# Memory tokens and the first key weights loaded in halves of the summed dimension, in a two-layer encoder step

## The reference

```python
def mem_kv(mem, norm_g, wk, wv, k_norm_g):
    bsz, m, _ = mem.shape
    hm = rmsnorm(mem, norm_g)
    mk = rmsnorm((hm @ wk).reshape(bsz, m, MEM_HEADS, MEM_HEAD_DIM), k_norm_g)
    mv = (hm @ wv).reshape(bsz, m, MEM_HEADS, MEM_HEAD_DIM)
    return mk, mv
```

## Time and profile before

| | us |
|---|---|
| median of 3 runs | 1813.92 |
| lowest, highest | 1813.88, 1814.5 |
| span of the profiled execution | 1812.1 |
| TensorE busy in it | 1766.3 (97%) |
| VectorE busy | 888.0 (49%) |
| ScalarE busy | 510.9 (28%) |
| GpSimd busy | 159.2 (9%) |

### The profile page before, as it was taken

One profiled execution on the slowest core, in us unless ns is written; L12 is line 12 of the kernel. 1 busy time (PEld: TensorE's weight loads), 2 busy tenths in 40 slices (PEclk: granted clock), 3 DMA queues, 4 the chain that ended last, 5 costly groups with the idle time before them and its releaser, 6 DMA issues.

```text
span 1812.1 us, 27654 instructions
## 1 busy us (share of the span) xinstructions
PE 1766.3 (97%) x11792; PEld 1608.6 (89%) x11792; DVE 888.0 (49%) x1398; ACT 510.9 (28%) x791; POOL 159.2 (9%) x153
## 2 busy tenths in 40 slices
PE   7999998999999999999999999899999999999997
PEld 6566556988999999999999997699799999999997
DVE  3699857557544323444335135644764442244431
ACT  4111254354322111122232144533442111111211
POOL 3011101221000000000023132100110000000000
PEclk9999999999999999999999998999999999999999
DMA  7222420251311122221223224213232112222120
GB/s 252 99 78 92 112 100 7 105 205 64 116 69 55 64 101 71 76 72 48 94 94 49 93 70 177 99 48 140 94 124 85 62 48 87 93 70 82 51 91 31
DMA packets 32059, 161.61 MB, mean 89 GB/s; under 512 B 8600, under 2 KB 9240, under 8 KB 18032
## 3 DMA queue, kind: packets, MB, share of 16 engines
q1 hardware_dynamic: 24032, 121.97, 20.1%
q0 software_dynamic: 7952, 38.60, 6.0%
HBM read 149.87 MB, written 10.42 MB: 88 GB/s over the span
## 4 chain that ended last, share of the span: by engine, by line
PE 93%; DVE 3%; ACT 1%; issue 1%; DMA 0%; POOL 0%; SPq 0%; DVEq 0%; ACTq 0%
PE G L798 88%; PE S L798 2%; PE Q L798 2%; PE Q L1408 1%; ACT work L1494 1%; ACT rstd L1494 0%; DMA ring<-in_w_mk 0%; DVE ev_low L2267 0%; DVE stats L2297 0%; PE Q L1205 0%; DVE stats L2563 0%; DVE work L2310 0%; DVE rstd L2018 0%; ACT mkT L1494 0%; ACT front L1494 0%
## 5 line engine op out<-in xcount | busy, mean ns | idle before, releaser
L798 PE MATMUL G<-h_split,w_split 128*128 128x320 f32 x5184 | 763.6, 309 | 0.0
L798 PEld LDWEIGHTS G<-h_split,w_split 128*128 128x128 f32 x5184 | 760.6, 188 | 0.2 <-issue 0.2
L1494 ACT ACTIVATE w_split<-ring 128x1024 fp32r<-128x1024 f32 (+2 forms) x172 | 165.0, 961 | 750.0 <-PE G L798 750.0
L798 PE MATMUL G<-g_split,w_split 128*128 128x320 f32 x2112 | 310.4, 309 | 0.0
L798 PEld LDWEIGHTS G<-g_split,w_split 128*128 128x128 f32 x2112 | 309.9, 188 | 0.0
L798 PE MATMUL G<-front,ring 128*128 128x128 f32 (+2 forms) x832 | 222.2, 428 | 11.2 <-DMA ring<-in_w_mk 9.4
L2033 DVE TENSOR_TENSOR w_split<-ring,w_split 128x1024 fp32r<-128x1024 f32 (+2 forms) x154 | 166.8, 1084 | 132.4 <-ACT w_split L1494 132.1
L798 PEld LDWEIGHTS G<-front,ring 128*128 128x128 f32 x832 | 132.2, 192 | 99.8 <-issue 96.0
L2410 DVE TENSOR_TENSOR work<-work,G 128x640 f32<-128x640 f32 x44 | 36.1, 821 | 204.1 <-PE G L798 204.1
L2108 DVE SCALAR_TENSOR_TENSOR front<-front,par 128x512 f32<-128x512 f32 x240 | 113.6, 547 | 0.1
L2401 DVE TENSOR_TENSOR work<-G,rstd 128x640 f32<-128x640 f32 x44 | 36.3, 824 | 128.7 <-PE G L798 116.2
(11 more groups left out here) (310 smaller groups left out, 1765.2 us busy)
## 6 DMA issues: line engine op xcount, KB each, us to landing
ring<-in_w_up0a SPq DMA_DIRECT2D x11, 1024.0 KB, 4.9
ring<-in_w_up0b SPq DMA_DIRECT2D x11, 1024.0 KB, 4.9
ring<-in_w_up1a SPq DMA_DIRECT2D x11, 1024.0 KB, 4.9
ring<-in_w_up1b SPq DMA_DIRECT2D x11, 1024.0 KB, 4.8
front<-in_mem_k POOLq DMA_DIRECT2D x8, 1024.0 KB, 7.2
front<-in_mem_v POOLq DMA_DIRECT2D x8, 1024.0 KB, 11.4
ring<-in_w_down0a SPq DMA_DIRECT2D x8, 704.0 KB, 4.0
ring<-in_w_down0b SPq DMA_DIRECT2D x8, 704.0 KB, 4.1
```

The costliest lines, as they stand in the source:

```text
L798: return nc.tensor.matmul(out, lhsT, rhs, start=start, stop=stop, **kw)
L1494: return nc.scalar.activation(*a, **k)
```

## The change

SyncE issues `par` first, then the first half of the tokens (steps 0 to 3) and the first half of key chunk 0 (the columns of the same steps, 4 KB per partition), then both second halves, then the early constants; x and the rest follow as before. The two halves of the tokens have semaphores of their own (`mem_in[0]`, `mem_in[1]`), the first half of the chunk has `half_in`, the second raises the chunk's usual one. TensorE runs the first four steps of tile 0 and of tile 1 when the first halves are there, then the last four of each. PSUM holds both tiles meanwhile. The wait for `ones` moves to the statistics after tile 1. ScalarE and VectorE wait for each half of the tokens when they come to it.

```diff
@@ SyncE
-            sp.dma_start(memx, dram["mem"]).then_inc(mem_in, 16)
+            def first_half(i):
+
+                ks = slice(4 * i, 4 * i + 4)
+                sp.dma_start(memx[:, ks], dram["mem"][:, ks]).then_inc(mem_in[i], 16)
+                at = slice(i * WCH // 2, (i + 1) * WCH // 2)
+                sp.dma_start(ring[:, 0, at], dram[CHUNKS[0][0]][0][:, at]).then_inc(chunk_in[0] if i else half_in, 16)
+
+            sp.dma_start(par[:, :], dram["par"]).then_inc(par_in, 16)
+            first_half(0)
+            first_half(1)
             sp.dma_start(const[:, 0:EARLY], dram["const"][:, 0:EARLY]).then_inc(ones_in, 16)
-            sp.dma_start(par[:, :], dram["par"]).then_inc(par_in, 16)
...
-            load(0, slice(0, 1), None)
             for k in range(0, KD, 2):
                 sp.dma_start(x[:, k:k + 2, :], dram["x"][:, k:k + 2, :]).then_inc(x_in[k // 2], 16)
             load(1, slice(1, 2), None)
@@ TensorE
-            pe.wait_ge(ones_in, 16)
...
+            def first_keys():
+
+                for half in range(2):
+                    if half:
+                        chunk(0)
+                    else:
+                        pe.wait_ge(half_in, 16)
+                    for n in range(2):
+                        out = G[n] if half else begin(n)
+                        for k in range(4 * half, 4 * half + 4):
+                            if n == 0:
+                                pe.wait_ge(mem_scaled, k + 1)
+                            m = mm(out[:, 0:MT], ring[:, 0, k * 256 + n * P:k * 256 + n * P + P], memh[:, 0, k, :],
+                                   k == 0, k == KD - 1)
+                        if half:
+                            m.then_inc(tile_done, 1)
+
             def memory_keys(l):
+                if l == 0:
+                    first_keys()
                 for n in range(4):
-                    if n % 2 == 0:
+                    if n % 2 == 0 and (l or n):
                         s = chunk(CHUNK[f"mk{l}"] + n // 2)
-                    project(TILE0[f"mk{l}"] + n, s, n % 2 * P, KD, lambda k: memh[:, l, k, :], width=MT,
-                            normed=1 if l and n == 0 else None, scaled=mem_scaled if l == 0 and n == 0 else None)
+                    if l or n >= 2:
+                        project(TILE0[f"mk{l}"] + n, s, n % 2 * P, KD, lambda k: memh[:, l, k, :], width=MT,
+                                normed=1 if l and n == 0 else None)
                     if l == 0 and n == 1:
+                        pe.wait_ge(ones_in, 16)
                         total = rstd[:, nstat[0] % 2, :]
@@ ScalarE
-            act.wait_ge(mem_in, 16)
             for k in range(KD):
+                act.wait_ge(mem_in[k // 4], 16)
                 square(memx[:, k, :], MT)
@@ VectorE
-            dve.wait_ge(mem_in, 16)
             for k in range(KD):
+                dve.wait_ge(mem_in[k // 4], 16)
                 v.tensor_scalar(memh[:, 0, k, :], memx[:, k, :], pr("mem0", k), None, ALU.mult).then_inc(mem_scaled, 1)
```

More of the change, by code:

```diff
@@ L484, in build @@
         h_hi, q_eps, silu = map(sem, ("h_hi", "q_eps", "silu"))
-        ones_in, const_in, par_in, mem_in, pads_in = map(
-            sem, ("ones_in", "const_in", "par_in", "mem_in", "pads_in"))
+        ones_in, const_in, par_in, half_in, pads_in = map(
+            sem, ("ones_in", "const_in", "par_in", "half_in", "pads_in"))
+        mem_in = [sem(f"mem_in{i}") for i in range(2)]
         x_in = [sem(f"x_in{i}") for i in range(KD // 2)]
@@ L808, in begin, with project @@
                 return G[n % 2]
-            def project(n, wslot, col, KT, rhs, cols=256, width=T, normed=None, halfway=None, scaled=None):
+            def project(n, wslot, col, KT, rhs, cols=256, width=T, normed=None, halfway=None):
                 out = begin(n)
@@ L817, in project @@
                         pe.wait_ge(applied, normed + k)
-                    if scaled is not None:
-                        pe.wait_ge(scaled, k + 1)
                     w = ring[:, wslot, k * cols + col:k * cols + col + P]
```

## The result

| | median us | lowest to highest | runs |
|---|---|---|---|
| before | 1814.01 | 1813.1 to 1817.44 | 18 |
| with the change | 1818.04 | 1815.64 to 1821.65 | 18 |

The ratio is 1.002, with an interval of 1.0013 to 1.0027: about 4 us slower, against a forecast of 1814.0 and a range up to 1816.0. The spread has grown too: 17 of the 18 runs of before lie within 1.7 us, those of the change over 6 us. The profiled execution has a span of 1816.2 us, 4.1 above that of before.

A forecast was written before the change was run, and what follows sets the result against it. The wait for value chunk 1, last late before 28.74 us in a backed-up load queue, was taken to absorb the earlier start. Span 1812.1 + 0.1 for halves = 1812.2, plus 1.8 from span to median: 1814.0 us, range 1812.2 to 1816.0.

The forecast's parts named there:

- The main step: At the first value product: TensorE waits for value chunk 1, landing at 28.6 us, so an earlier start gains nothing.
- the cost of halves in the queue: Loads at the start: halves cost -0.6 to +0.4 us, taken as +0.1, going straight into value chunk 1's landing.
- The sentence on the skill's rule: Load queue: the skill's about 2 us per transfer has no room as a serial cost; x's four parts took 6.37 us.
- The start: First product of key tile 0: at 6.5 us (6.2 to 7.5) instead of 9.42, with 1152 KB less ahead of it.
- I keep 8.83 us: First two key tiles: the same 16 steps keep their slow start-up and take 8.83 us, 6.5 to 15.3.
- the lead: TensorE's gain on the kernel before: 2.9 us at tile 1, 1.6 at key tile 2, zero at the value products.
- The gap: TensorE's idle time ahead of the first value product, waiting for value chunk 1: 2.4 us in place of 0.97.
- The clock: Rival: longer idle before 28.7 us may halve TensorE's granted clock, costing 1.65 us, to 1815.7; chance 0.10.
- the row at 42.8 us: Profile of the kernel before: after a single 1.8 us idle ahead of 42.88 us the granted clock stayed at 1.00.
- The rival on each transfer's cost: Rival: two more transfers in the queue put the end up to 3.2 us later, 1817.1, or 1817.5; chance 0.03.
- SyncE's two more issues: Ahead of x and later loads: 0.44 us each, so these are issued 0.9 us later, costing nothing.
- the earlier issue of `glu`: Next weight chunk after tile 1: issued at 15.3 us in place of 18.28, still behind the value chunks, costing nothing.

The follow-up runs named there:

- filler: Changed kernel with four extra products, results unused, in TensorE's idle time ahead of the value products: 1816.17 us.
- after_repeat: The changed kernel run once more, nothing altered: 1818.72 us, ratio 1.0018 to the kernel before.
- whole_4k_rows: order_only with tokens and key chunk 0 in one transfer each, cut into 256 rows of 4 KB by the DRAM layout: 1814.10 us.
- order_only: Kernel before with the change's order of loads alone, tokens and key chunk 0 whole, no halves: 1813.91 us, ratio 0.9998.
- late_halves: order_only with key chunk 1, not chunk 0, in two half transfers at every other 4 KB of DRAM: 1814.95 us.
- halves_contiguous: Changed kernel with tokens and key chunk 0 laid out in DRAM so each half is one unbroken 512 KB piece: 1815.25 us.

## Why the prediction was wrong

**The main step held.** "Whatever it does earlier ends in this same wait": with value chunk 1 ahead of x the gap vanished in all four runs with that move, and only then did an earlier first product bring the statistic of x forward with it.

**The step that failed is the cost of halves in the queue**, -0.6 to +0.4 us. It measured +1.57 at the value products in the profiled execution and more in the others (filler 2.0, after_repeat 2.9), and +2.3 in the median of the runs with a mean granted clock of 0.995 or more. I priced the halves by the length of a row alone, from whole loads with rows of 5 and 3.6 KB; whole_4k_rows shows that this comparison was right and beside the point. Transfers were counted at nothing, from x in four parts at full rate, but those were parts of a load that was in four parts anyway, each with its own rows side by side. That a half reads every other 4 KB of the array was in the diff, and no row of before has such a load; it should have kept a bound of its own. The sentence on the skill's rule went too far as well: a serial 2 us for each transfer is not seen, but splitting did cost with unbroken halves too, 0.23 and 0.47 MB in two executions. And a loss in bytes was the only kind I looked for: that a part of each load falls behind (1.9 us between first and last completion, against 0.8 in order_only) stood in no term.

**The start.** Expected 6.5 (6.2 to 7.5), measured 8.34 and 9.62 in two executions: a term mis-sized by the same cause, as the bytes ahead were taken at 400 a us and came at 176 to 254 (86 to 217 in the second). "I keep 8.83 us" for the products was off as well. They took 9.78, and 8.6 to 10.1 in the other runs: the slow records at the head are a different number each time. So tile 1 was done at 18.12 against a forecast of 15.3, and the lead was 0.1 us and not 2.9.

**The gap** was foreseen as 2.4 us and measured as 2.23, for another reason: not TensorE early, but value chunk 1 late.

**The clock** was a rival at 0.10, with 1.65 us to pay and the place named. It came: 1.69 us between 30 and 46 us in the profiled execution. I placed a gap of 2.4 us after dense work nearer to the row at 42.8 us, where the clock had stayed; the runs show that at 2.2 us it goes either way and that at 3.0 it fell. Ten of 18 runs of the change and seven of 11 of after_repeat have a mean granted clock of 0.994 or lower, so a chance near one half would have fitted. The price was about right: 1.69 us traced, 2.0 between the medians of the runs with and without the fall.

**The range** held the rivals one at a time. The two that came about add up, since a later landing is what makes the gap in which the clock falls: 1814.0 + 1.5 + 1.7 = 1817.2 by the profiled execution, and 1814.0 + 2.3 + 2.0 = 1818.3 by the medians; 1818.04 was measured. The rival on each transfer's cost, 1817.1 to 1817.5, came near in time but not in kind.

**Others.** SyncE's two more issues, the moved wait for `ones`, the added waits of ScalarE and VectorE and the earlier issue of `glu` cost nothing that the traces show, as forecast; the last wasn't even earlier (18.15 against 18.28).

## What to carry to other kernels

Before a first wait is shortened, look for the last transfer that the same engine waits for: if the queue is full up to it, only that transfer's place in the queue counts, and moving it forward costs one line. Splitting a load is not free even where its rows are long enough: what has to be asked is how many transfers it adds and what each reads of the array, and halves should be laid out whole in DRAM. A gap of 2 us ahead of TensorE can cost as much again in its clock, in some runs and not in others, so a change that lengthens one has two prices that go together.

## What the runs showed of the hardware

- Transfers of 64 partitions moved 169 to 262 GB/s at a DMA share near 1.0, those of 128 partitions 400 to 430.
- Halves of 512 KB in alternating 4 KB pieces moved 86 to 258 GB/s between 4 and 7 us in five executions with the change's order of loads, 311 to 361 at 15 to 17 us in late_halves, and 414 to 415 from 7 to 10 us in one execution of the changed kernel (320, then 406 to 414 in the other).
- The last of a load's 16 completion steps came 0.6 to 1.0 us after the first behind whole loads, and 1.8 to 2.6 us behind two pairs of halves in the change's order or grouped.
- After 2.2 us without work TensorE's granted clock fell to 0.50, from 30.8 to 34.1 us, in one execution of the changed kernel and stayed at 1.00 in the other and in halves_contiguous; after 3.03 us it fell, after 0.61 to 1.64 it stayed.
- The kernel before loses 3.7 us in 14 of 143 runs, with a mean granted clock of 0.993 in place of 0.995 to 0.997.
- The first products after the start run slowly at a granted clock that the rows call 1.00: the same 32 records took from 8.6 to 10.1 us in all.
